# Expert stage of a two-block model: indexed gathers and stores of filled slots only, and a down projection in three products of rounded parts

## The reference

```python
# h (1024 tokens, 1024 wide); 32 experts, top 2 of each token, width 512
slot_tok = full(n_blocks * 128, n).at[dest].set(token)      # each expert's slots padded to whole blocks of 128
xb = h_pad[slot_tok].reshape(n_blocks, 128, 1024)           # an empty slot reads a row of zeros
yb = (silu(xb @ w_gate[e]) * (xb @ w_up[e])) @ w_down[e]    # one block of slots, one expert
y  = segment_sum(yb * slot_w, slot_tok)                     # token = sum of its two slots, weighted
x  = x + gate_f * y
```

## Time and profile before

| | |
|---|---|
| Median of 3 runs | 4797.4 us (4794.48 to 4807.75) |
| Profiled execution, its own time | 4787.98 us |
| Its span (first to last instruction) | 4786.2 us |
| Busy share PE / DVE / ACT / POOL | 84% / 46% / 31% / 18% |
| Moved by the DMA engines | 495.45 MB |

### The profile page before, as it was taken

The page is one execution under the profiler, slowest core; times in us unless marked ns, Lnnn a source line. Parts: engine busy times, 40 slices in busy tenths (PEclk is TensorE's granted clock), DMA queues, the critical chain, the costliest instruction groups (busy, mean ns, idle before and its releaser), DMA issues. The chain is left out here.

```text
span 4786.2 us, 43613 instructions
## 1 busy us (share of the span) xinstructions
PE 4001.8 (84%) x16492; PEld 2893.1 (60%) x16492; DVE 2180.9 (46%) x2605; ACT 1463.4 (31%) x2334; POOL 875.9 (18%) x380
## 2 busy tenths in 40 slices
PE   6699779997689689988575989898999854999995
PEld 6578545556577445556363866576777644666663
DVE  0274356662355366741346623234452212666665
ACT  1311235551201144440114135412221011555541
POOL 0143210001143400003130102043333331000001
PEclk6799879997899889989798999999999975999997
DMA  4111112222211101113121212043333232999995
GB/s 158 61 32 33 33 41 83 84 79 75 87 37 38 42 27 58 62 58 106 23 31 53 53 33 23 14 75 75 81 94 71 69 125 73 364 379 381 380 336 215
DMA packets 367554, 495.45 MB, mean 104 GB/s; under 512 B 47645, under 2 KB 222978, under 8 KB 366850
## 3 DMA queue, kind: packets, MB, share of 16 engines
q1 hardware_dynamic: 354578, 448.27, 31.2%
q0 software_dynamic: 7888, 26.78, 1.5%
q10 hardware_dynamic: 4896, 17.83, 0.9%
HBM read 408.38 MB, written 84.44 MB: 103 GB/s over the span
## 5 line engine op out<-in xcount | busy, mean ns | idle before, releaser
L1091 PE MATMUL values<-probs,vp 128*128 128x512 f32 x672 | 348.9, 601 | 12.1 <-issue 6.4
L1180 ACT ACTIVATE probs<-scores 128x512 f32<-128x512 f32 (+1 forms) x336 | 196.0, 583 | 309.4 <-PE scores L211 307.7
L1389 POOL TENSOR_TENSOR out_hi<-out_w,ones 128x1024 fp32r<-128x1024 f32 x24 | 57.3, 2387 | 1193.6 <-DMA out_w<-in_w_out 1193.6
L209 PE MATMUL scores<-q_hi,k_rest 97*128 97x512 f32 (+1 forms) x336 | 262.5, 781 | 0.0
L678 DVE SCALAR_TENSOR_TENSOR conv_out<-conv_in,vectors,conv_out 128x1295 f32<-128x1295 f32 (+1 forms) x120 | 254.5, 2121 | 4.3
L3249 PE MATMUL dp<-h_t,abt 128*128 128x512 f32 x544 | 241.9, 597 | 1.8 <-ACT abt L3298 1.8
L209 PE MATMUL gates_ps<-x_t_r,gates_w_r 128*128 128x512 f32 (+1 forms) x560 | 210.2, 375 | 22.0 <-POOL gates_w_r L259 22.0
L209 PE MATMUL out_ps<-h_t_r,out_w_r 128*128 128x512 f32 (+1 forms) x448 | 172.3, 385 | 67.2 <-POOL out_w_r L1391 67.2
L3280 ACT ACTIVATE expert_hi<-wu 128x1024 fp32r<-128x1024 f32 x136 | 144.8, 1065 | 247.3 <-PE gp L211 247.3
L1262 DVE TENSOR_REDUCE mx<-made 128x1 f32<-128x640 f32 (+1 forms) x272 | 203.8, 794 | 27.0 <-PE made L1032 26.4
L209 PE MATMUL smb<-x_t_r,merge_w_r 128*128 128x512 f32 x480 | 197.3, 411 | 18.6 <-POOL merge_w_r L2614 15.9
(11 more groups left out here) (519 smaller groups left out, 9827.1 us busy)
## 6 DMA issues: line engine op xcount, KB each, us to landing
wg<-in_w_gate SPq DMA_DIRECT2D x34, 2048.0 KB, 10.6
wu<-in_w_up SPq DMA_DIRECT2D x34, 2048.0 KB, 11.9
h_t<-in_w_down SPq DMA_DIRECT2D x34, 2048.0 KB, 10.4
slot_rows<-zero_rows SPq DMA_DIRECT2D x16, 1536.0 KB, 9.4
ahead_w<-in_w_ada SPq DMA_DIRECT2D x48, 512.0 KB, 3.8
slot_rows<-yb ACTq DMA_DIRECT2D x34, 512.0 KB, 8.4
gates_w<-in_w_in SPq DMA_DIRECT2D x28, 512.0 KB, 4.0
mod_w<-in_w_mod SPq DMA_DIRECT2D x12, 1024.0 KB, 5.2
```

Source lines behind the costliest of these rows:

```text
L209: nc.tensor.matmul(out, lhs[1], rhs[0], start=start, stop=False, **kw)
L1091: nc.tensor.matmul(O[b % 2][:, 0:w], vp[g // 2 % 2][:, kb, g % 2 * VD:g % 2 * VD + P], pr[m % 3][:, 0:w], start=kb == 0, stop=kb == nk - 1 ...
L1180: nc.scalar.activation(pr[m % 3][:, 0:w], S[m % 2][:, 0:w], ACT.Exp, scale=scale).then_inc(s.exped, 1)
L1389: nc.gpsimd.tensor_tensor(hi[:, c, :, :], wt[:, c, :, :], all_ones(k), ALU.mult).then_inc(s.split, 1)
```

## The change

- **Routing**: the table has two numbers per slot, the token (for the gather) and the row of the output to write (token, or token + 1024 for a token's second slot). Empty slots hold 2048.
- **Gather**: indices above 1023 are left out, so empty slots move nothing. The buffers are set to zero once by POOL.
- **Store**: the ACT-issued store of 128 rows is gone. POOL issues an indexed scatter of the filled rows to a buffer of 2048 rows.
- **Down projection**: 8 plain float32 products (16 passes) become 8 `split_matmul` calls, 24 products. ACT rounds the down weights in four pieces of 128x1024 (`round_down`, in its step between the SiLU and piece 0 of the next block), POOL takes their four rests (`rest_down`), ACT rounds the activations (`keep_a`, now to a_hi), and DVE takes their rest (`rest_a`, behind `multiply`). PE's `down` waits for the rest of each piece, and `keep_rows` copies after all of them.
- **Combination**: plain loads of 128 rows from each half of the buffer, four buffers of two, all issued by POOL. The multiplication by the first weight moves from DVE to ACT.
- **Attention**: the clearing, its buffer and its waits are gone.

```diff
-                if zero is not None and n % 3 == 2:
...
-                        sp.dma_start(dst, zero[:, :].unsqueeze(1).broadcast_to([P, m, 512])).then_inc(s.rows_cleared, 16)
...
-                                            tok[:, t:t + 1], None).then_inc(s.scattered, 16)
+                                            tok[:, t, 2 * i:2 * i + 2], None).then_inc(s.scattered, 16)
...
+            wd_rest = [flat_h_r[:, u * FK * D:(u + 1) * FK * D].rearrange("p (k n) -> p k n", n=D) for u in range(2)]
+            wd_hi = [flat_h_r[:, (2 * FK + j) * D:(2 * FK + j + 1) * D].rearrange("p (c n) -> p c n", n=CTX) for j in range(2)]
+            wd_hi += [k.x_r[:, 4 * j:4 * j + 4, 0:CTX] for j in range(2)]
...
                 def gather(u, at):
                     pool.indirect_dma_start(xb[u][:, :], None, r.rows,
-                                            bass.IndirectOffsetOnAxis(ap=at.bitcast(U32), axis=0)).then_inc(gathered[u], 16)
+                                            bass.IndirectOffsetOnAxis(ap=at.bitcast(U32), axis=0),
+                                            bounds_check=SEQ - 1, oob_is_err=False).then_inc(gathered[u], 16)
+
+                def scatter(u, at):
+                    pool.indirect_dma_start(r.out_rows, bass.IndirectOffsetOnAxis(ap=at.bitcast(U32), axis=0),
+                                            yb[u][:, :], None, bounds_check=2 * SEQ - 1, oob_is_err=False)\
+                        .then_inc(stored[u], 16)
+
...
+                def rest_down(b, u):
+                    for j in range(FK):
+                        pool.wait_ge(s.down_hi, count(b, FK, j + 1))
+                        nc.gpsimd.tensor_tensor(pieces(wd_rest[u], j), pieces(wd[u], j), wd_hi[j].bitcast(F32),
+                                                ALU.subtract).then_inc(s.down_rest, 1)
 
                 for b in range(FIXED + 1):
                     if b >= 2:
                         pool.wait_ge(s.xt_made, 2 * (b - 1))
-                    gather(b % 2, idx[:, b:b + 1])
+                    gather(b % 2, idx[:, b, 0:1])
+                    if b >= 4:
+                        pool.wait_ge(s.d_kept, 2 * (b - 3))
+                        scatter(b % 2, idx[:, b - 4, 1:2])
+                    if b >= 3:
+                        rest_down((None, b - 3), (b - 3) % 2)
...
                 def down(b, u):
                     pe.wait_ge(s.a_kept, count(b, 1, 1))
-                    pe.wait_ge(down_in[u], count(b, 8, 16 - 8 * u))
-                    for half in range(2):
-                        if later(b):
-                            pe.wait_ge(s.d_kept, count(b, 2, half - 1))
-                        for j in range(FK):
-                            m = nc.tensor.matmul(dp[half][:, :], at[:, j, :], wd[u][:, j, half * 512:(half + 1) * 512],
-                                                 start=j == 0, stop=j == FK - 1)
-                        m.then_inc(s.d_made, 1)
+                    for j in range(FK):
+                        pe.wait_ge(s.down_rest, count(b, FK, j + 1))
+                        for half in range(2):
+                            if j == 0 and later(b):
+                                pe.wait_ge(s.d_kept, count(b, 2, half - 1))
+                            cols = slice(half * 512, (half + 1) * 512)
+                            m = split_matmul(nc, dp[half][:, :], (at_hi[:, j, :], at_rest[:, j, :]),
+                                             (wd_hi[j][:, 2 * half:2 * half + 2, :], wd_rest[u][:, j, cols]),
+                                             start=j == 0, stop=j == FK - 1)
+                        m.then_inc(s.down_used, 1)
...
                 def keep_a(b):
                     act.wait_ge(s.a_made, count(b, 1, 1))
                     if later(b):
-                        act.wait_ge(s.d_made, count(b, 2, 0))
-                    nc.scalar.activation(at[:, :, :], ap[:, :, :], ACT.Copy).then_inc(s.a_kept, 1)
-
-                def store(b, u):
-                    turn, base = b
-                    rows = base * P if turn is None else turn * (2 * P) + base * P
-                    act.wait_ge(s.d_kept, count(b, 2, 2))
-                    act.dma_start(r.out_rows[bass.ds(rows, P), :], yb[u][:, :]).then_inc(stored[u], 16)
+                        act.wait_ge(s.down_used, count(b, FK, 0))
+                    nc.scalar.activation(at_hi[:, :, :], ap[:, :, :], ACT.Copy).then_inc(s.a_hi, 1)
+
+                def round_down(b, u):
+                    act.wait_ge(down_in[u], count(b, 8, 16 - 8 * u))
+                    for j in range(FK):
+                        if later(b):
+                            act.wait_ge(s.down_used, count(b, FK, j + 1 - FK))
+                        nc.scalar.activation(wd_hi[j], pieces(wd[u], j), ACT.Copy).then_inc(s.down_hi, 1)
...
-                def step(this, before, after, next_weights, last, u):
-                    round_weights(this, u, 4)
-                    if last:
-                        store(last, u)
-                    for p in range(5, 8):
+                def step(this, before, after, next_weights, u):
+                    for p in range(4, 8):
                         round_weights(this, u, p)
                     gate(this)
+                    if before:
+                        round_down(before, 1 - u)
                     if next_weights:
                         for p in range(3):
                             round_weights(after, 1 - u, p)
...
+                def rest_a(b):
+                    dve.wait_ge(s.a_hi, count(b, 1, 1))
+                    nc.vector.tensor_tensor(at_rest[:, :, :], ap[:, :, :], at_hi[:, :, :].bitcast(F32), ALU.subtract)\
+                        .then_inc(s.a_kept, 1)
+
                 def keep_rows(b, u):
                     if later(b, 1):
                         dve.wait_ge(stored[u], count(b, 8, -8 * u))
+                    dve.wait_ge(s.down_used, count(b, FK, FK))
                     for half in range(2):
-                        dve.wait_ge(s.d_made, count(b, 2, half + 1))
                         nc.vector.tensor_copy(yb[u][:, half * 512:(half + 1) * 512], dp[half][:, :]).then_inc(s.d_kept, 1)
...
                     multiply(this, u)
+                    if before:
+                        rest_a(before)
                     rest_x(after)
                     if next_weights:
                         take_rest(after, 1 - u, 3)
...
             for t in range(NT2):
-                if t >= 2:
-                    pool.wait_ge(s.out_ready, t - 1)
-                for i in range(2):
-                    pool.indirect_dma_start(y[t % 2][i][:, :], None, r.out_rows,
-                                            bass.IndirectOffsetOnAxis(ap=r.slot[:, i, t:t + 1].bitcast(U32), axis=0))\
-                        .then_inc(gathered[t % 2], 16)
+                if t >= HELD:
+                    pool.wait_ge(s.out_ready, t - HELD + 1)
+                pool.dma_start(y[t % HELD][:, :, :], r.out_rows.rearrange("(i n) d -> n i d", i=2)[t * P:(t + 1) * P, :, :])\
+                    .then_inc(rows_in[t % HELD], 16)
...
+            for t in range(NT2):
+                first = y[t % HELD][:, 0, :]
+                act.wait_ge(rows_in[t % HELD], 16 * (t // HELD + 1))
+                nc.scalar.activation(first, first, ACT.Copy, scale=r.weight[:, 0, t:t + 1]).then_inc(s.weighed, 1)
...
-                a, b = y[u][0][:, :], y[u][1][:, :]
-                dve.wait_ge(gathered[u], 32 * (t // 2 + 1))
-                step(nc.vector.tensor_scalar(a, a, r.weight[:, 0, t:t + 1], None, ALU.mult))
+                a, b = y[t % HELD][:, 0, :], y[t % HELD][:, 1, :]
+                dve.wait_ge(rows_in[t % HELD], 16 * (t // HELD + 1))
+                dve.wait_ge(s.weighed, t + 1)
                 step(nc.vector.scalar_tensor_tensor(a, b, r.weight[:, 1, t:t + 1], a, ALU.mult, ALU.add))
                 step(nc.vector.tensor_tensor(a, a, gate[:, :], ALU.mult))
```

More of the change, by code:

```diff
@@ L863, in _, with attention @@
                         .then_inc(s.normed, 1)
-def attention(nc, k, a, l, last, cq, ckv, kr, ahead, to_clear):
+def attention(nc, k, a, l, last, cq, ckv, kr, ahead):
     scale = float(QK) ** -0.5
@@ L963, in _ @@
                 sp.dma_start(wa[n % 2][:, :], w_next[:, c, c0:c0 + AHEAD]).then_inc(ahead_in[n % 2], 16)
-                if zero is not None and n % 3 == 2:
-                    if n == 2:
-                        sp.wait_ge(s.set_once, ONCE)
-                    rows = to_clear.rearrange("(b p) d -> p b d", p=P)
-                    m = to_clear.shape[0] // P // HEADS
-                    for side in range(2):
-                        dst = rows[:, n // 3 * m:(n // 3 + 1) * m, side * 512:(side + 1) * 512]
-                        sp.dma_start(dst, zero[:, :].unsqueeze(1).broadcast_to([P, m, 512])).then_inc(s.rows_cleared, 16)
-                        cleared += 16
-            if cleared:
-                sp.wait_ge(s.rows_cleared, cleared)
         @block.gpsimd
@@ L1455, in first_layer @@
```

(26 more changed lines are left out.)

72 lines of the change are left out of this document (39 added, 33 removed).

## The result

The kernel with the change takes 5106.99 us (median of 4 runs, 5103.01 to 5110.03), the kernel before 4800.08 us (4794.48 to 4807.75): a ratio of 1.0642, 95% interval 1.0628 to 1.0655. The forecast was 5086 us with a range of 5010 to 5150.

What follows compares the result with a forecast made beforehand. PE was taken to bound the kernel at 19.35 us per expert step. Steps +299, last scatter +2 and combination -12 on 4788.0 gave 5077, and the median's 9.4 us offset made it 5086 us, range 5010 to 5150.

Steps and rivals of the forecast that it cites:

- PE stops being the bound and waits for `a_rest`: Expert steps: `down` waits for DVE's rest of the activations until t = 21.7, leaving PE idle 9.1 us per step.
- ACT's order: Expert step on ACT: four down roundings from t = 7.2 to 11.1, three gate roundings to 14.1, a_hi at 14.7.
- The alternation: Before `down`: DVE's three gate rests and POOL's subtractions take turns, 7.8 us from t = 12.5 to 20.3.
- The clock: Down products after PE's gap: PE's clock falls and costs 2.1 us per step, bounds 0 and 2.4.
- The step: Experts: 21.7 + 5.54 + 2.1 = 29.3 us against 19.35, +9.95 us in each of 30 steps, +299 us.
- Combination: Combination stage: four buffers remove waits for gathers and ACT takes over a multiplication, -12 us, between -8 and -14.
- the last scatters: End of the last block: the last scatter, issued by POOL behind a copy of indices, costs +2 us.
- Gathers, stores, routing and clearing at nothing: Fewer bytes, hidden scatter and gather, dropped store issue, small routing operations and the removed clearing: 0 us.
- The sum: Whole kernel: +299 + 2 - 12 = +289 us on the profiled 4788.0, so 5077 us.
- With the clock held: Expert steps: VectorE and GpSimd alternate but PE's clock stays up, 27.2 us a step, 5023 us; chance 9%.
- second rival: Expert steps: VectorE and GpSimd do not hinder each other, 22.7 or 24.8 us a step, 4885 or 4950 us; chance 5%.
- The rival of the whole-instruction hold: Expert steps: each subtraction holds VectorE throughout and the slow stretch is longer, 31.05 us a step, 5138 us; chance 12%.

## Why the prediction was right, and by how much off

- **PE stops being the bound and waits for `a_rest`**: right. Predicted start of `down` t = 21.7, measured 22.0 in steps 2 to 28 (23.7 in step 1, 25.1 and 22.3 in steps 30 and 32). ACT's order came as worked out: roundings from t = 7.2, POOL's first subtraction at 8.4 (predicted 8.3), DVE's first gate rest at 12.1 (12.2).
- **The alternation**: right in kind. The three rests were to end at 20.3 and ended at 20.8. A subtraction in between adds 2.15 us to a rest (3.37 - 1.22), between the 2.02 taken from the earlier trace rows and the 2.39 of a whole subtraction. The rule of the Trainium skill that the prediction names ("SBUF — State Buffer", "Who interferes with whom") would give the whole 2.39, and the measured 2.15 is 0.2 less. The second subtraction, which I had through when DVE arrived, was not: 0.86 us more. I had put the first two at 2.1 us each, though the earlier trace rows gives 2.385 for one alone, and 8.3 + 2 x 2.385 is already 13.1. So the close agreement at the end is partly luck: the rests took 8.66 us and not 7.8, but began at 12.1 and not at 12.5. `multiply` and `rest_a` overlap their neighbours a little and take 1.25 us.
- **The clock**: right. 2.1 us were taken with 2.4 as the upper bound; the kernel with PE kept busy gives 2.2 as the mean, above the bound in single steps. Single steps lose 1.3 to 2.7, so the slow stretch is not the fixed 4 to 5.3 us that I read from one place.
- **The step**: predicted 29.3, measured 29.97 in steps 1 to 28, and 33.06 and 29.75 in steps 30 and 32. This is the term that was mis-sized: 0.3 us ahead of `down` (22.0 for 21.7), and 0.3 from its first product to the next step (8.0 for 7.64). About half of the second is not the clock: with the clock at 1.00 that stretch is 27.77 - 22.05 = 5.72 us, where I took 5.54. Why step 30 is 3.3 us longer than step 32 is not shown. The stretch grew by 320.3 us instead of 299. Steps 29 and 31 together changed by -0.1 us, as predicted.
- **Combination**: predicted -12, measured 7 x 1.63 = -11.4. The end behind the last block gained 7.6 in all, so the last scatters cost nearer 4 than the 2 us I gave them: from the last copy of rows to the combination's first transfer it is 11.3 us in place of 7.8.
- **Gathers, stores, routing and clearing at nothing**: right by the kernel with plain products, which gains 8 us where the combination alone explains as much.
- **The sum**: +289 predicted against +322.0 of the profiled executions: 21 from the steps, 2.4 from the end, 9.3 from an earlier start of the experts in the profile of before. By medians the change costs 306.9 us.
- **One reading of the rows was wrong**, without weight for the sum: something does wait for ACT in the kernel before. DVE's gate rests wait 10.0 us for it between 4100 and 4600 us, and its up rests 56.3 us.
- **The rivals**: without contention I gave 24.8 us a step with the clock's loss and a start near 17.1; the run without subtractions gives 24.0 and 16.8. With the clock held I gave 27.2, and measured 27.8. They were close prices for what did not happen. The "+98 in all" of that second rival is its steps alone; with the -10 of the rest it is +88, as its 4885 us has it. The rival of the whole-instruction hold had the mechanism nearly right and the price too high, since only two whole subtractions and the tail of one stand in the chain.

## What to carry to other kernels

Before giving GpSimd work because it sleeps, lay its start and end beside VectorE's instructions that read two SBUF tensors: each holds the other up, so add the durations up. Here that, a queue order and the fall of the clock made a down projection that is 1 us cheaper for TensorE cost 10.6 us a step. Put the operations that a product waits for ahead of those for a later block in every engine's queue. Then see whether the two engines still have room together, and split only as many pieces as they have room for.

Compare variants by the length of a step as well as by their total: stages that no edit touches moved by up to 37 us here.

## What I had not expected

- GpSimd that only writes does not slow VectorE's subtractions at all (1219 ns with POOL busy 55% of the time), against 2355 ns with reads.
- A gather's issue on POOL takes 1.84 us beside the gate rests, and 1.97 us with the subtractions left out. It takes 1.02 us with memsets in their place, when it starts behind those rests, and 0.94 us in the kernel before. In the change and in the kernel without subtractions DVE's rest ends 0.93 and 1.09 us into the gather, and the remaining 0.9 us are what it costs alone. So the gather's issue seems to be held as a subtraction is; no run separates this further.
- A gap of 4.3 us in each step already brings the clock down for part of the next products (6.8 to 7.0 us for 5.5), while PE's waits of 1.7 us a step for the up rests, in pieces, leave it at 1.00.
- A step's loss of clock repeats in fours, from 1.3 to 2.7 us, at gaps of equal length (9.4 us).
- Ten, or nine, more constant products in one stage came with 37, or 21, us in stages before it.
